# A residual block on one core: RMSNorm scales moved behind the projections, x in column blocks, early transposes of the second norm

## Chip, cores and metric

One core of one Trainium2 chip runs the whole block in one launch. The metric is the device time of the launch in microseconds (us), the median of three runs.

## The reference

`x` is 256 rows (tokens) by 2048 columns, float32.

```
n1   = rmsnorm(x) * g1
proj = n1 @ w_in            # q k v o (4 x 1024), i f (8), x_r g_r (2 x 1024)
A    = sigmoid(o) * headnorm(mlstm(q, k, v, i, f))       # 4 heads x 256
B    = rglru(conv4(x_r)) * gelu(g_r)                     # 8 blocks x 128
x    = x + [A, B] @ w_out
n2   = rmsnorm(x) * g2
gate, up = split(n2 @ w_up)                              # 2 x 5632
x    = x + (silu(conv3(gate)) * up) @ w_down
y    = rmsnorm(x) * g3
```

`rmsnorm(x)` is `x * r`, with one number `r = 1/sqrt(mean(x*x) + eps)` per row. Since `r` belongs to a row of x and not to a column of a weight, `(r*x*g) @ w` equals `r * ((x*g) @ w)`.

## The kernel before

Each float32 operand is used as a rounded part (`hi`) and a rest (`lo`). A 512 KB block of weights (a *unit*) lands in one of four slots of `raw`; ScalarE rounds it into `w[..., 0, :]` (`round_units`), VectorE subtracts to get `w[..., 1, :]` (`split_units`, L550), and TensorE multiplies (`unit`, L946 and L948: one 512-wide and one 256-wide matmul for each pair, 8 pairs in a unit). Four units make a *group*: 256 output columns over the whole depth of 2048. SyncE loads the next unit into a slot as soon as its split is done.

The order of the work on every engine is written out by hand; semaphores that count the named steps of an engine (`Steps`, `after`, `did`) tie them together, and each engine works its own list strictly in order. So what stands behind a waiting instruction waits too.

**Start.** SyncE loads x in five row pieces, then weights. ScalarE squares each piece with a running sum (`squares`), and takes the root of it (`std`); VectorE takes the reciprocal (`norm_scale`) and writes `xn = x * r` (`normalise`, L587). TensorE meanwhile multiplies ones 29 times (L971), then transposes `xn` in eight banks of four 128x128 blocks (`transpose_bank`, L927): banks 0 to 3 ahead of the first group, 4 to 7 inside it (`first_group`). ScalarE and VectorE evacuate each bank as `hi` and `lo` with the gain g1 (`transposed_hi`, `transposed_lo`, L593). Then come group 0 (q), the gate columns i and f (L978, 16 matmuls), and group 1 (k).

**Gate chain.** From the gate columns VectorE and ScalarE compute the running sums and maxima of the gates on 4 rows: `gate_bias`, `gate_sum` (L643), `f_neg`, `f_abs` on VectorE; `f_exp`, `f_ln` on ScalarE, each behind a load of its function table; then on VectorE `logf`, the scan `fsum`, `gdif` (TensorE transposes it, L984), the scan `cmax`, `neg_M`, `neg_m`, `neg_clip`. Only behind `neg_clip` does VectorE's list have the splits of group 2, the v columns of head 0 (L942 on TensorE).

**Heads.** Four rounds of six groups (v, o, x_r, g_r, next q, next k). After each group the two parts are added (`copy_half` on ScalarE, `add_half` L561 on VectorE). The last head's final steps run beside the first units of the output projection.

**Output projection and second norm.** `contraction` runs two halves of the 2048 output columns; a half is four *bodies* of four units (L1051, 12 matmuls for each unit). In PSUM, half 0 uses banks 4 to 7, half 1 banks 0 to 3. VectorE adds the result to x (`add_residual`, L794: `out0_0`, `out1_0` after half 0; `out0_1`, `out1_1`, `out1_2` after half 1). Then the same norm, scaling and transposing as at the start, and the first group of the up projection. Its 22 rounds have two groups each, `gate_post` (conv on VectorE, L845 and L849, silu on ScalarE) and `up_post` (L856).

Of the kernel before, what the change touches and what calls it, by code (L numbers as in the profile page):

```python
# [89 lines left out]
WARM_UP = 29  # L90
# [19 lines left out]
def hybrid_block(nc, x, w_in, w_out, w_up, w_down, wa, wx, gate_w, par_in, const_in, gfin_in, out):  # L110
    with ExitStack() as ctx:
# [3 lines left out]
        def sb(name, shape, dt=F32, where=ctx):  # L115
# [14 lines left out]
        ones = sb("ones", [P, P])  # L130
        ident = cst[:, C_ID:C_ID + P]
# [13 lines left out]
        decay = sb("decay", [P, 3 * P], where=mixer)  # L145
        pT = sb("pT", [P, 3 * P], where=mixer)
# [43 lines left out]
        x_landed = {(r, n): sem(f"x_landed{r}_{n}") for r in range(ROWS) for n in range(len(PIECES[r]))}  # L190
        par_landed = sem("par_landed")
        gate_landed = sem("gate_landed")
# [15 lines left out]
        stats_act = "warm sq0_0 sq1_0 sq0_1 std0 "  # L208
        norm_dve0 = "rstd0 xn0_0 xn0_1 xn0_2 xn0_3 "
        norm_dve1 = "rstd1 xn1_0 xn1_1 xn1_2 "  # L210
        tr_steps = " ".join(f"t{b}" for b in range(KT // 2)) + " "
        norm_act = "sq1_1 sq1_2 std1 t0 t1 t2 t3 xn1_3 t4 t5 t6 t7 "
        out_steps = "out0_0 out1_0 base out0_1 "
        A0 = Steps(act_step, 0, stats_act + norm_act + "gw_hi lam_exp lam_ln gate_half f_exp f_ln floor")
        V0 = Steps(dve_step, 0, "start gw_zero base rstd0 xn0_0 xn0_1 base1 xn0_2 xn0_3 " + norm_dve1 + tr_steps + "gw_lo lam_neg lam_abs lam_relu softplus c_col"
                   " half_bias nc_col hg gate_bias gate_sum f_neg f_abs logf fsum gdif cmax neg_M neg_m neg_clip gcol0 gcol1 pads")
        E0 = Steps(pe_step, 0, tr_steps + "gates gcol0 gcol1")
        A1 = Steps(act_step, A0.end(), "decay hsq rms_std o_tanh r_tanh0 r_tanh1 i_tanh0 i_tanh1 lru_a0 lru_a1 lru_t0 lru_t1 lru_s g_tanh")
        V1 = Steps(dve_step, V0.end(), "arg0 arg1 pT dneg den dsq hvar"
                   " conv0_0 conv1_0 conv0_1 conv1_1 conv0_2 conv1_2 conv0_3 conv1_3 rstd og mix0 mix1"  # L220
                   " ux asq w u scan0 scan1 gsq gp gq gh mixl")
        E1 = Steps(pe_step, E0.end(), "scores pv rms lru")
        L1 = Steps(pool_step, 0, "mask0 mask1 nsq")
        EO = Steps(pe_step, E1.end(H), "row0_0 row0_1 row1_1")
        A2 = Steps(act_step, A1.end(H), stats_act + norm_act)
        V2 = Steps(dve_step, V1.end(H), out_steps + norm_dve0 + "out1_1 out1_2 base1 " + norm_dve1 + tr_steps + "fpad")
        E2 = Steps(pe_step, EO.end(), tr_steps)
        A3 = Steps(act_step, A2.end(), "silu")
        V3 = Steps(dve_step, V2.end(), "c0_0 c1_0 c0_1 c1_1 c0_2 c1_2 act")
        ED = Steps(pe_step, E2.end(), "row0_0 row0_1 row1_1")  # L230
        A4 = Steps(act_step, A3.end(UP_ITERS), stats_act + "y0_0 y0_1 sq1_1 sq1_2 std1 y1_0 y1_1")
        V4 = Steps(dve_step, V3.end(UP_ITERS), out_steps + "rstd0 y0_2 y0_3 out1_1 out1_2 base1 rstd1 y1_2 y1_3")
        L4 = Steps(pool_step, L1.end(H), "xg0 xg1")
# [20 lines left out]
        def _(sp):  # L254
            for r, n in ((0, 0), (1, 0), (0, 1), (1, 1), (1, 2)):
                lo, hi = PIECES[r][n]
                sp.dma_start(xres[:, r, lo:hi], x[0, r * P:(r + 1) * P, lo:hi]).then_inc(x_landed[r, n], 16)
# [9 lines left out]
            def load_group(group, view, col):  # L267
                for s in range(RING):
                    load(group, s, view[s, :, :, bass.ds(col, COLS)],
                         raw[:, s, :].rearrange("p (c n) -> p c n", c=CH))  # L270
# [25 lines left out]
            load_group(0, in_v, COL_Q)  # L296
# [21 lines left out]
        def _(act_e):  # L318
# [20 lines left out]
            def squares(A, r, n, V=None):  # L339

                if V:
                    after(act_e, V, f"out{r}_{n}")
                else:
                    act_e.wait_ge(x_landed[r, n], 16)
# [13 lines left out]
            def stats(A, V, r, source=None):  # L358

                for n in range(1, len(PIECES[r])):  # L360
                    squares(A, r, n, source)
                std(A, V, r)
# [4 lines left out]

            def normalise(A, c):

                cols = slice(c * BANK, (c + 1) * BANK)  # L370
                did(act_fn(xn[:, 1, cols], xres[:, 1, cols], scale=small[:, RSTD + 1:RSTD + 2]), A, f"xn1_{c}")
# [10 lines left out]
            def normalised_hi(A, V, E, gains, prepare):  # L382

                for s in range(RING):
                    prepare(s)
                    if s == 2:
                        after(act_e, V, "rstd1")
                        normalise(A, 3)
                    transposed_hi(A, E, gains, 2 * s)
                    transposed_hi(A, E, gains, 2 * s + 1)  # L390

            after(act_e, V0, "start")
            warm_sqrt(A0)
            for r in range(ROWS):
                squares(A0, r, 0)
            for r in range(ROWS):
                stats(A0, V0, r)
            act_e.wait_ge(par_landed, 32)
            normalised_hi(A0, V0, E0, PAR_GMIX, lambda s: round_units(0, [s]))
            act_e.wait_ge(gate_landed, 16)  # L400
            after(act_e, V0, "gw_zero")
            did(act_fn(gws[:, :, 0:2, 0:H], gw[:]), A0, "gw_hi")

# [4 lines left out]
            round_units(1)  # L408
            copy_half(0, 0, qT[:])
# [76 lines left out]
            def contraction(src, first_group, bodies, A, V):  # L486

                for half in range(2):
                    base = first_group + half * bodies + 1
                    if half == 1 or src is not mixT:  # L490
                        for s in range(RING):
                            round_units(base, [s])
                            round_tiles(src, RING, [s])
# [631 lines left out]
```

## Time and profile before

| | |
|---|---|
| median of three runs | 1156.99 us (1156.61 to 1157.96) |
| span of the profiled execution, first to last instruction | 1146.2 us |
| TensorE busy | 1129.4 us, 99% |
| VectorE busy | 725.4 us, 63% |
| ScalarE busy | 585.5 us, 51% |
| GpSimd busy | 17.4 us, 2% |
| moved by DMA | 213.55 MB, mean 186 GB/s |
| ScalarE function table loads | 25, 1283 ns each |

The runs are timed from outside and are 10.8 us longer than the span of the profiled execution, for which no outside time of its own is given. A busy TensorE here means that matmuls are under way, not that they run at the full clock: PEclk in the profile tells the clock that it was granted, 1.00 for 2.4 GHz and 0.50 for 1.2 GHz. The idle time of an engine only matters where TensorE waits for it.

### The profile page before, as it was taken

To read this page: it belongs to the slowest core of one execution; us is meant where nothing else is said; L and a number is where in the kernel's file an instruction comes from. 1 tells how busy PE (TensorE), PEld (TensorE's weight loads), DVE (VectorE), ACT (ScalarE), POOL (GpSimd) and SP (SyncE) were. 2 spreads that over 40 slices of the span, in tenths; PEclk is the share of its full clock that TensorE was granted. 3 is DMA by queue.
4 is the path that set the end of the run, shared out by engine and by line. 5 is a ranking of instruction groups with operands and counts; after the bars stand their busy time and mean duration, and the time that the engine had idled before them with its cause. 6 is when DMAs were issued, how large, how long until landed. Compare 5 with 4: busy or idle time off the path is not lost.

```text
span 1146.2 us, 18127 instructions
## 1 busy us (share of the span) xinstructions
PE 1129.4 (99%) x6052; PEld 976.8 (85%) x6052; DVE 725.4 (63%) x956; ACT 585.5 (51%) x767; POOL 17.4 (2%) x27
## 2 busy tenths in 40 slices
PE   8999999999999999999999999999999999999997
PEld 7888888888888888888888888888888888888885
DVE  6659576585785586666656656666665755556554
ACT  6647465474665564445444444444444554555454
POOL 0000000000000000000000000000000000002000
PEclk8999999999999999999999999999999999999999
DMA  7665757657565546655665666566565566665653
GB/s 229 197 191 172 196 148 209 165 155 204 183 209 193 167 147 203 194 188 172 207 189 165 212 189 184 180 202 187 168 214 187 193 190 196 189 196 186 195 190 109
DMA packets 165592, 213.55 MB, mean 186 GB/s; under 512 B 6764, under 2 KB 148076, under 8 KB 165440
## 3 DMA queue, kind: packets, MB, share of 16 engines
q1 hardware_dynamic: 164944, 210.79, 59.7%
q0 software_dynamic: 624, 2.45, 0.6%
q8 instruction: 14, 0.23, 0.1%
q14 instruction: 10, 0.08, 0.0%
HBM read 211.10 MB, written 2.11 MB: 186 GB/s over the span
## 4 chain that ended last, share of the span: by engine, by line
PE 97%; ACT 1%; DVE 1%; DMA 1%; issue 0%; DVEq 0%; SPq 0%; ACTq 0%
PE ps L946 41%; PE ps L1051 27%; PE ps L948 21%; PE ps L942 3%; PE ps L944 1%; PE ps L927 1%; DMA xres<-x_dram 1%; PE ps L1022 1%; ACT xn L322 0%; PE ps L978 0%; ACT w L322 0%; PE ps L1004 0%; PE ps L994 0%; DVE aT L556 0%; DVE xn L587 0%
## 5 line engine op out<-in xcount | busy, mean ns | idle before, releaser
L946 PE MATMUL ps<-xT,w 128*128 128x512 f32 x2048 | 716.8, 394 | 0.0
L550 DVE TENSOR_TENSOR w<-raw,w 128x1024 fp32r<-128x1024 f32 x392 | 475.1, 1224 | 366.3 <-ACT w L322 365.5
L322 ACT ACTIVATE w<-raw 128x1024 fp32r<-128x1024 f32 x392 | 411.7, 1058 | 424.7 <-PE ps L948 260.1
L948 PE MATMUL ps<-xT,w 128*128 128x256 f32 x2048 | 573.5, 280 | 0.0
L946 PEld LDWEIGHTS ps<-xT,w 128*128 128x128 f32 x2048 | 384.1, 188 | 85.6
L948 PEld LDWEIGHTS ps<-xT,w 128*128 128x128 f32 x2048 | 387.5, 189 | 0.3
L1051 PE MATMUL ps<-w,aT 128*128 128x512 f32 x1440 | 327.1, 389 | 0.4 <-DVE aT L556 0.4
L1051 PEld LDWEIGHTS ps<-w,aT 128*128 128x128 f32 x1440 | 270.1, 188 | 57.0 <-DVE aT L556 0.9
L322 ACT ACTIVATE fs<-fc 128x512 f32<-128x512 f32 x22 | 13.9, 632 | 86.5 <-DVE fc L849 86.5
L942 PE MATMUL ps<-w,xT 128*128 128x512 f32 x128 | 45.1, 397 | 0.0
L556 DVE TENSOR_TENSOR aT<-act,aT 128x256 fp32r<-128x256 f32 x88 | 39.0, 443 | 0.0
L849 DVE SCALAR_TENSOR_TENSOR fc<-fg,par,fc 128x256 f32<-128x256 f32 x88 | 36.7, 479 | 0.0
L944 PE MATMUL ps<-w,xT 128*128 128x256 f32 x128 | 35.7, 279 | 0.0
L322 ACT ACTIVATE aT<-act 128x256 fp32r (+1 forms) x88 | 35.3, 401 | 0.0
L322 ACT ACT_TABLE_LOAD x25 | 32.1, 1283 | 1.2 <-PEq L1116 0.8
L942 PEld LDWEIGHTS ps<-w,xT 128*128 128x128 f32 x128 | 24.0, 188 | 5.8
L944 PEld LDWEIGHTS ps<-w,xT 128*128 128x128 f32 x128 | 24.1, 188 | 0.0
L322 ACT ACTIVATE xn<-xres 128x1024 f32<-128x1024 f32 (+1 forms) x15 | 13.3, 884 | 19.3 <-DVE xres L794 13.7
L845 DVE TENSOR_SCALAR fc<-fg,par 128x256 f32<-128x256 f32 x44 | 16.2, 410 | 5.9 <-DVE fg L561 5.8
L856 DVE TENSOR_TENSOR act<-fu,fs 128x512 f32 (+1 forms) x22 | 15.2, 693 | 4.9 <-DVE fu L561 4.8
L927 PE MATMUL ps<-cst,xn 128*128 128x128 f32 x64 | 10.9, 336 | 7.0 <-DVE xn L587 7.0
L322 ACT ACTIVATE xT<-ps,par 128x256 fp32r<-128x256 f32 x32 | 12.8, 475 | 8.2 <-PE ps L927 8.2
(131 smaller groups left out, 362.9 us busy)
## 6 DMA issues: line engine op xcount, KB each, us to landing
raw<-w_up_dram SPq DMA_DIRECT2D x176, 512.0 KB, 4.5
raw<-w_in_dram SPq DMA_DIRECT2D x96, 512.0 KB, 3.8
raw<-w_down_dram SPq DMA_DIRECT2D x88, 512.0 KB, 4.6
raw<-w_out_dram SPq DMA_DIRECT2D x32, 512.0 KB, 4.7
y_dram<-xn SPq DMA_DIRECT2D x8, 256.0 KB, 3.0
xres<-x_dram SPq DMA_DIRECT2D x3, 512.0 KB, 6.8
bc<-rows POOLq DMA_DIRECT2D x4, 256.0 KB, 5.4
gfin<-gfin_dram POOLq DMA_DIRECT2D x1, 1024.0 KB, 9.1
```

The costliest lines, as they stand in the source:

```text
L322: return sc.activation(out_, in_, fn, **kw)
L550: v.tensor_tensor(w[:, s, :, 1, :], raw[:, s, :].rearrange("p (c n) -> p c n", c=CH), w[:, s, :, 0, :], ALU.subtract).then_inc(lo_ready, 1)
L556: v.tensor_tensor(aT[:, s, 1, :], src[:, bass.ds(first + s, 1), :].rearrange("p a n -> p (a n)"), aT[:, s, 0, :], ALU.subtract).then_inc(a ...
L845: did(v.tensor_scalar(fc[:, b, :], tap, fpar(b, k), fpar(b, FTAPS), ALU.mult, ALU.add), V3, f"c{b}_{k}")
L849: did(v.scalar_tensor_tensor(out=fc[:, b, :], in0=tap, scalar=fpar(b, k), in1=fc[:, b, :], op0=ALU.mult, op1=ALU.add), V3, f"c{b}_{k}")
L856: did(v.tensor_tensor(act[:, bass.ds(j * 2, 2), :], fu[:], fs[:], ALU.mult), V3, "act")
L927: ins = nc.tensor.transpose(ps[:, 4 + b % 4, n * S + r * P:n * S + (r + 1) * P], xn[:, r, kt * P:(kt + 1) * P], ident)
L942: mm(full, xT[:, kt, 0, cut], w[:, s, c, :, :].rearrange("p a n -> p (a n)"), start=kt == 0, stop=False)
L944: ins = mm(rest, xT[:, kt, 1, cut], w[:, s, c, 0, :], start=False, stop=kt == KT - 1)
L946: mm(full, w[:, s, c, 0, cut], xT[:, kt, :, :].rearrange("p a n -> p (a n)"), start=kt == 0, stop=False)
L948: ins = mm(rest, w[:, s, c, 1, cut], xT[:, kt, 0, :], start=False, stop=kt == KT - 1)
L1051: ins = mm(ps[:, bank0 + 2 * r + n, :], aT[:, s, a_part, cut], w[:, s, 2 * n:2 * n + 2, w_part, :], start=opens and s == 0 and a_part == 0 ...
```

## The change

1. x comes in four column blocks of 512 columns, both halves of the rows in one 512 KB transfer, alternating in SyncE's list with the four units of group 0. The identity matrix and the parameters are issued by ScalarE and no longer by GpSimd; the triangular mask is loaded apart.
2. TensorE transposes `xres` (x itself) as each block lands; 8 in place of 29 matmuls of ones stand ahead. The squares come after the rounding of group 0 on ScalarE, and `r` is ready later.
3. `r` is spread to all partitions by two matmuls of ones with a diagonal matrix (`diagonals`, `spread_rows`, into `rB`): in the middle of group 1, and after the first group of the up projection.
4. The projection outputs are multiplied by `r`: q and k through the decay mask (`rmask`, one GpSimd product of 384 columns for two of 128), v in its two evacuations (now two pieces each), o on GpSimd (`o_r`), x_r and g_r on VectorE (`xr_r`, `gr_r`, 128x512), the gates by `gate_r` and `gate_b`; in the up projection the gate columns on VectorE (`fr`, 128x512) and the up columns through silu's output on GpSimd (`fs_r`).
5. Before the second norm, banks 0 to 3 are transposed after body 1 of half 1, the first rows of banks 4 to 7 inside its last body, their second rows after the first unit of the up projection.

```diff
-WARM_UP = 29
+WARM_UP = 8
...
-            load_group(0, in_v, COL_Q)
+            load_group(0, in_v, COL_Q, load_x)
...
+            def diagonals(A, V):
+                for r in range(ROWS):
+                    after(dve, A, f"std{r}")
+                    did(v.reciprocal(small[:, RSTD + r:RSTD + r + 1], small[:, STD + r:STD + r + 1]), V, f"rstd{r}")
+                for r in range(ROWS):
+                    after(dve, V, f"rstd{r}")
+                    did(v.tensor_scalar(diag[:, r, :], ident, small[:, RSTD + r:RSTD + r + 1], None, ALU.mult), V, f"diag{r}")
+            def row_scales(V, E):
+                after(dve, E, "rB")
+                did(v.tensor_copy(rB[:, 0, :], ps[:, B_DEN, 0:S]), V, "rB")
+                after(dve, V, "rB")
...
+            transpose_x(0)
+            transpose_x(1)
+            pe.wait_ge(group_free, 1)
+            unit(0, 0, 0, tiles=V0)
+            transpose_x(2)
+            unit(0, 1, 0, tiles=V0)
+            transpose_x(3)
+            unit(0, 2, 0, tiles=V0)
+            unit(0, 3, 0, tiles=V0)
...
+            for s in range(RING):
+                unit(1, s, 1)
+                if s == 1:
+                    spread_rows(V0, E0)
...
+                did(v.tensor_tensor(xr[:, :, TAPS - 1:], xr[:, :, TAPS - 1:], rB[:].to_broadcast([P, 2, S]), ALU.mult), V1, "xr_r")
...
+                did(v.tensor_tensor(gr[:], gr[:], rB[:].to_broadcast([P, 2, S]), ALU.mult), V1, "gr_r")
...
+                did(v.tensor_tensor(fg[:, :, FTAPS - 1:], fg[:, :, FTAPS - 1:], rB[:].to_broadcast([P, 2, S]), ALU.mult), V3, "fr")
...
+            with pool.Fori(0, UP_ITERS) as j:
+                after(pool, A3, "silu", j)
+                did(nc.gpsimd.tensor_tensor(fs[:], fs[:], rB[:].to_broadcast([P, 2, S]), ALU.mult), L3, "fs_r")
...
+            contraction(G_OUT, OUT_BODIES, 0, G_OUT, E2, transpose_early, transpose_late)
+            after(pe, V2, "out0_1")
+            unit(G_UP, 0, 0, tiles=V2)
+            after(pe, V2, "out1_2")
+            for b in range(4, 8):
+                did(transpose_bank(b, [1]), E2, f"t{b}")
+            for s in range(1, RING):
+                unit(G_UP, s, 0, tiles=V2)
+            spread_rows(V2, E2)
```

Two places show how the order moves. First VectorE in the gate chain. Before, behind the splits of group 1 (L550; L561 adds q's two parts, L640 and L643 are the gate sums):

```order
L550 TENSOR_TENSOR w<-raw,w 128x4x256 x4
L561 TENSOR_TENSOR qT<-ps,qT 128x512
L640 SCALAR_TENSOR_TENSOR grow<-ps,par,grow 64x256
L643 TENSOR_TENSOR grow<-ps,grow 64x256
L645 TENSOR_SCALAR gtmp<-grow 4x256
L647 TENSOR_TENSOR gtmp<-gtmp,grow 4x256
```

and in the changed kernel, where L572 is the split, L583 the add, L608 the copy of `rB`, L660 to L664 the first steps on the recurrence's parameters, whose result ScalarE waits for:

```order
L572 TENSOR_TENSOR w<-raw,w 128x4x256 x2
L583 TENSOR_TENSOR qT<-ps,qT 128x512
L608 COPY rB<-ps 128x256
L651 TENSOR_SCALAR rmask<-rB,small 128x256
L652 TENSOR_SCALAR rmask<-rB,small 128x128
L656 TENSOR_TENSOR rmask<-rmask,cst 128x128 x2
L660 TENSOR_SCALAR lp<-par 128x8
L662 TENSOR_TENSOR lp<-lp,par 128x8
L664 TENSOR_SCALAR lp<-lp 128x8
L668 TENSOR_TENSOR grow<-ps,grow 64x256
L670 TENSOR_TENSOR grow<-ps,grow 64x256
L672 TENSOR_TENSOR grow<-grow,rB 64x256
```

The gate sums now stand behind the copy of `rB`, five operations of the mask and three on parameters; the splits of group 2 stand behind all of them, as before.

Second, TensorE around the end of the output projection. Before, half 1 ends with its last body (L1051), and all first 16 transposes (L927) follow it:

```order
L1068 COMPARE_AND_BRANCH
L1051 MATMUL ps<-w,aT 128x512 x48
L927 MATMUL ps<-cst,xn 128x128 x16
L946 MATMUL ps<-xT,w 128x512
L948 MATMUL ps<-xT,w 128x256
```

In the changed kernel L1125 is the projection and L985 the transpose:

```order
L1125 MATMUL ps<-w,aT 128x512 x144
L985 MATMUL ps<-cst,xres 128x128 x16
L1145 UNCONDITIONAL_BRANCH
L1125 MATMUL ps<-w,aT 128x512 x48
L1145 REGISTER_ALU
L1145 COMPARE_AND_BRANCH
L1125 MATMUL ps<-w,aT 128x512 x36
L985 MATMUL ps<-cst,xres 128x128 x8
L1125 MATMUL ps<-w,aT 128x512 x12
L1011 MATMUL ps<-xT,w 128x512
L1013 MATMUL ps<-xT,w 128x256
```

Sixteen transposes stand two bodies earlier, eight inside the last body, and the first unit of the up projection (L1011, L1013) follows the projection directly.

## Rows read from the trace of the kernel before

**Rows 1.** Waits of TensorE: engine, line, what for: us in total, times, longest.

```profile
PE ps L927 <- DVE xn L587: 7.0, 2, 4.2
```

**Rows 2.** Timeline, TensorE, start: start us, us, line, operation, count [idle before <-releaser].

```profile
14.46 3.65 PE L927 MATMUL ps<-cst,xn 128*128 128x128 f32 x16 [4.25 <-DVE xn L587]
...
18.54 0.63 PE L946 MATMUL ps<-xT,w 128*128 128x512 f32 x1
...
19.18 0.52 PE L946 MATMUL ps<-xT,w 128*128 128x512 f32 x1
...
21.39 1.04 PE L927 MATMUL ps<-cst,xn 128*128 128x128 f32 x8
22.18 0.47 PE L946 MATMUL ps<-xT,w 128*128 128x512 f32 x1
...
31.51 3.83 PE L978 MATMUL ps<-xT,gws 128*128 128x512 f32 x16
35.18 0.39 PE L946 MATMUL ps<-xT,w 128*128 128x512 f32 x1
```

**Rows 3.** Timeline, ScalarE, start: squares of x, then one evacuation and one rounding.

```profile
8.02 1.06 ACT L322 ACTIVATE xn<-xres 128x1024 f32<-128x1024 f32 x1 [1.42 <-DMA xres<-x_dram]
...
10.20 1.06 ACT L322 ACTIVATE xn<-xres 128x1024 f32<-128x1024 f32 x1 [1.03 <-DMA xres<-x_dram]
...
22.03 1.57 ACT L322 ACTIVATE xT<-ps,par 128x256 fp32r<-128x256 f32 x4 [0.79 <-PE ps L927]
23.47 1.07 ACT L322 ACTIVATE w<-raw 128x1024 fp32r<-128x1024 f32 x1
```

**Rows 4.** Stretches of the windows view: PE, PEld, DVE, ACT, POOL busy; PEclk; DMA share; GB/s.

```profile
12.20:12.70 0.50, 0.00 (x0) 0.00 (x0) 0.50 (x2) 0.50 (x3) 0.00 (x0) 0.91 1.11 350
19.40:19.90 0.50, 0.50 (x4) 0.42 (x4) 0.50 (x3) 0.50 (x2) 0.00 (x0) 0.97 0.02 4
408.00:409.00 1.00, 1.00 (x6) 0.85 (x5) 1.00 (x2) 1.00 (x3) 0.00 (x0) 0.72 0.92 292
```

**Rows 5.** Timeline, ScalarE, gate chain.

```profile
38.39 0.42 ACT L322 ACTIVATE gtmp<-gtmp 4x256 f32<-4x256 f32 x1 [1.34 <-DVE gtmp L647]
38.83 1.28 ACT L322 ACT_TABLE_LOAD   x1
```

**Rows 6.** Timeline, VectorE, gate chain and the splits behind it.

```profile
37.16 0.43 DVE L643 TENSOR_TENSOR grow<-ps,grow 64x256 f32<-64x256 f32 x1
...
43.86 3.48 DVE L550 TENSOR_TENSOR w<-raw,w 128x1024 fp32r<-128x1024 f32 x3
```

**Rows 7.** Timeline, TensorE, first group of head 0.

```profile
46.58 0.50 PE L942 MATMUL ps<-w,xT 128*128 128x512 f32 x1
```

**Rows 8.** Timeline, TensorE, end of the output projection and second norm.

```profile
398.72 3.11 PE L1051 MATMUL ps<-w,aT 128*128 128x512 f32 x13
404.57 0.63 PE L927 MATMUL ps<-cst,xn 128*128 128x128 f32 x4 [2.74 <-DVE xn L587]
...
420.90 0.39 PE L946 MATMUL ps<-xT,w 128*128 128x512 f32 x1
```

**Rows 9.** Timelines, last head: the tile that the second body needs, and the projection.

```profile
324.27 0.42 DVE L556 TENSOR_TENSOR aT<-mixT,aT 128x256 fp32r<-128x256 f32 x1
...
314.57 15.64 PE L1051 MATMUL ps<-w,aT 128*128 128x512 f32 x68
```

**Rows 10.** VectorE groups by shape: busy us, mean ns, idle before.

```profile
L760 DVE TENSOR_TENSOR gr<-gr 128x512 f32<-128x512 f32 x4 | 2.8, 693 | 0.1
```

**Rows 11.** Timelines, GpSimd beside VectorE in the down projection.

```profile
1033.91 5.75 POOL L910 TENSOR_TENSOR xn<-xres,gfin 128x1024 f32<-128x1024 f32 x2 [741.61 <-ACT xn L322]
...
1037.32 2.63 DVE L556 TENSOR_TENSOR aT<-act,aT 128x256 fp32r<-128x256 f32 x1
```

**Rows 12.** Timelines, up projection: VectorE splits and ScalarE rounding.

```profile
450.47 3.50 DVE L550 TENSOR_TENSOR w<-raw,w 128x1024 fp32r<-128x1024 f32 x3 [1.65 <-ACT w L322]
...
454.38 1.06 ACT L322 ACTIVATE w<-raw 128x1024 fp32r<-128x1024 f32 x1 [1.71 <-PE ps L948]
```

More of the change, by code:

```diff
@@ new lines, in hybrid_block @@
+        A0 = Steps(act_step, 0, "warm " + early + "t4 t5 gw_hi t6 t7 " + x_squares + "gate_half lam_exp lam_ln f_exp f_ln floor")
+        V0 = Steps(dve_step, 0, "start gw_zero " + early + "t4 t5 gw_lo t6 t7 base base1 " + rows + "rm0 rm1 tri0 tri1"
+                   " lam_neg lam_abs lam_relu gate_mid gate_sum gate_r gate_b f_neg f_abs softplus c_col"
+                   " half_bias nc_col hg logf fsum gdif cmax neg_M neg_m neg_clip gcol0 gcol1 pads")
+        E0 = Steps(pe_step, 0, early + late + "gates rB gcol0 gcol1")
@@ L222, in hybrid_block @@
         E1 = Steps(pe_step, E0.end(), "scores pv rms lru")
[L223 to L227, printed above, removed]
+        L1 = Steps(pool_step, 0, "mask o_r nsq")
+        E2 = Steps(pe_step, E1.end(H), "row0_0 " + early + "row0_1 row1_1 " + late + "rB")
@@ L228, in hybrid_block @@
+        A2 = Steps(act_step, A1.end(H), "warm sq0_0 sq1_0 " + early + "sq0_1 sq1_1 sq1_2 " + late + "std0 std1")
+        V2 = Steps(dve_step, V1.end(H), "out0_0 out1_0 " + early + "base out0_1 out1_1 out1_2 base1 fpad " + late + rows)
         A3 = Steps(act_step, A2.end(), "silu")
-        V3 = Steps(dve_step, V2.end(), "c0_0 c1_0 c0_1 c1_1 c0_2 c1_2 act")
+        V3 = Steps(dve_step, V2.end(), "fr c0_0 c1_0 c0_1 c1_1 c0_2 c1_2 act")
+        L3 = Steps(pool_step, L1.end(H), "fs_r")
         ED = Steps(pe_step, E2.end(), "row0_0 row0_1 row1_1")
-        A4 = Steps(act_step, A3.end(UP_ITERS), stats_act + "y0_0 y0_1 sq1_1 sq1_2 std1 y1_0 y1_1")
@@ L484, in _, with prepare_body @@
             head(H - 1, True)
+            def prepare_body(src, group, first):
+                for s in range(RING):
+                    round_units(group, [s])
+                    round_tiles(src, first, [s])
             def contraction(src, first_group, bodies, A, V):
@@ L489, in contraction @@
                     base = first_group + half * bodies + 1
[L490 to L493, printed above, removed]
+                    prepare_body(src, base, RING)
                     if half == 1:
@@ L1067, in contraction @@
                     body(0, opens=True)
-                    with pe.Fori(1, bodies - 1) as b:
+                    if half == 1 and early:
+                        body(1)
+                        early()
+                    with pe.Fori(2 if half == 1 and early else 1, bodies - 1) as b:
                         body(b)
```

316 lines of the change are left out of this document (179 added, 137 removed).

## Prediction

> **What bounds the kernel now.** I read the waits of TensorE first. It is busy for 99% of the span and waits for work twice, 7.0 us together, both times for a normalised x to transpose: 4.2 us at the start, 2.7 us at the second norm [rows 1, 8]. Nearly everything between is a queue of matmuls without a gap. So work added on VectorE, ScalarE or GpSimd costs only where TensorE comes to wait for it, and there are three places to look at: the start, the gate chain, the second norm. Second I read the timelines of these places, third the granted clock in the windows view. TensorE waited from 10.2 to 14.46; from about 12.6 its clock was 1.2 GHz, half of the full one (mean 0.91 of a stretch of 0.5 us), and it came back only at about 19.4, some 4.9 us after work began again [rows 2, 4]. At half clock a pair of matmuls takes 0.64 us (18.54 to 19.18), at full clock 0.35; a unit of 8 pairs is 2.8 us (group 1 and the two small gcol transposes run from 35.18 to 46.58) [rows 2, 7]. At the second norm the clock fell again and was back at about 408.5, 4.0 us after the restart at 404.57 (0.72 as the mean of 408 to 409) [rows 4, 8].
>
> **Start.** Removed from the path: squares, root and scaling, between the last piece of x and the first transposes. Their place is taken by the landing of column blocks 0 and 1. SyncE now has block 0, a unit of weights, block 1 in its list. The second and third 512 KB pieces landed at 8.02 and 10.20 before [rows 3]; block 1 is the third, so I take 10.20. TensorE then has 8 transposes at half clock (half of 16 in 3.65: 1.8 us), to 12.0. It is unit 0's turn, long rounded and split. The clock should be back 4.9 us after 10.2, at 15.1: five pairs of 0.64, three of 0.35, to 16.3. Eight warm transposes are 0.8 us (21.39 to 22.18) [rows 2], to 17.1; unit 1 to 19.9; the last transposes to 20.7; unit 2 to 23.5. Unit 3 waits a little: bank 6 is there at 20.3, its and bank 7's evacuation takes 1.57 us, the rounding 1.07 [rows 3], the split 1.2 [rows 6], to 24.1. Unit 3 ends at 26.9, the 16 gate matmuls take 3.7 us (31.51 to 35.18), and group 1 begins at 30.6 in place of 35.18 [rows 2]: **4.6 us earlier**. The 21 matmuls of ones that go cost nothing where they stood, but the clock is no longer full at 10.2; that is in the sum, since the first transposes were slow before as well. The transfers move four blocks past units of weights; block 3, now the seventh of eight pieces, is not wanted before 19.9, so the four pieces after the third have 9.7 us.
>
> **Gate chain.** Here the change adds a wait. `rB` comes out of TensorE between units 1 and 2 of group 1: 5.6 us after its start, and about 0.4 for the two small matmuls, so at 36.6. Call this R. It needs `diag1`: ScalarE is through with unit 3 at about 23, has three 1.06 us squares, two of 0.6, two roundings and two roots to do, some 8.5 us, and `diag1` follows at about 32.3, 4 us early. Behind R stand in VectorE's list: the copy (0.43, as L643 [rows 6]), four operations for the mask (0.3 each), two small ones (0.2 each): 2.0 us. Then ScalarE: `lam_exp`, table load 1.28, `lam_ln`, table load 1.28, to R + 5.0; the gate sums on VectorE, six operations of about 0.43, are done at R + 4.6. From the start of `f_exp` to the end of the first split of group 2 it was 6.7 us (38.39; first of three splits from 43.86, 1.2 us) [rows 5, 6], and this piece is unchanged. So the first unit of head 0 can start at R + 11.7 = 48.3, while TensorE is through with group 1 at R + 5.6. Before, it started at 46.58 [rows 7] without a wait. The lead of 4.6 us is gone and **1.7 us are lost** on top. The wait is 6.1 us, broken only by two tiny transposes when `gdif` comes; the clock fell in the shorter waits, so it falls here, and 4.0 to 4.9 us at half clock cost 2.0 to 2.5: **2.2 us**. Who else waits: ScalarE's `floor` and GpSimd's `bc` transfers come about 3 us later, but `arg0`, which wants them, follows TensorE's own delay of 3.9.
>
> The page "ScalarE: Activation LUTs" of the Trainium skill, What ACT_TABLE_LOAD costs, gives about 1.28 us for a load plus about 1.38 for a drain. By the page, the three loads of this chain behind R would cost 4.1 us more. The trace speaks against it: `f_exp` ends at 38.81 and the load begins at 38.83 [rows 5]. I take 1.28 alone.
>
> **Heads.** v: two pieces for one, 0.3 us on VectorE; the mask: one GpSimd operation for two; both end 7 us before TensorE asks. `o_r` on GpSimd has a whole group of 11 us. `xr_r` and `gr_r` are 0.69 us each [rows 10] and 0.7 with their wait, 1.4 a head. In three heads VectorE's list has idle places that take in the first, and the next splits come about a microsecond ahead. In the last head it runs without a pause into the output projection: the tile for body 1 was ready at 324.69, would be at 326.1, and TensorE wants it at 325.6 (48 matmuls of 0.23 us behind 314.57) [rows 9]. **0.5 us lost**; bounds 0 and 1.4.
>
> **Second norm.** From the last projection matmul (401.83) to the second group of the up projection (420.90) it was 19.1 us [rows 8]. Of the new list, all of this stands on TensorE: 32 transposes at full clock, 3.2; four units, 11.2; two matmuls for `rB`, 0.4; 14.8 in all. Gaps should not come: `out1_0` is long done when body 1 ends; `out0_1` (1.2 us) has two half units, 2.7 us; `out1_2` is covered by the first unit, 2.8 us, and banks 4 to 7 are evacuated beside unit 1. **4.3 us gained**; the lower bound, with half a unit of gap, is 2.9.
>
> **Up projection.** `fr` adds 0.7 us to VectorE in each of 22 rounds. The split of the first unit of the next even group ended at 451.7 and TensorE took it at about 454.4 (the end of a group, which ScalarE's rounding at 454.38 waited for) [rows 12]; 2.0 us of 2.7 stay. `fs_r` on GpSimd begins when silu ends and is wanted by `act` more than 6 us later. Two GpSimd products of 1024 columns took 5.75 us, 2.9 each; a 512-wide one is some 1.4 by that. A VectorE subtraction beside them took 2.63 us in place of 0.42, and ended when GpSimd did [rows 9, 11]. So `fs_r` may hold up a split by 0.3 us, since the rounding before it takes 1.1 of the 1.4. Zero cost. The Trainium skill's page "SBUF — State Buffer", Who interferes with whom, calls this an exclusive lock of the port pair that GpSimd shares with VectorE, held for an instruction; the trace agrees, 2.63 us for 0.42.
>
> **Sum.** +1.7 + 2.2 + 0.5 - 4.3 = +0.1 us on the span of 1146.2. The runs' median is 10.8 us above the span, and nothing outside the span changes: 1156.99 + 0.1 = **1157.1 us**. Two large gains and two large losses cancel, so the error of each stays in full. A measurement of this kernel tells 0.2%, 2.3 us, from no change.
>
> **Rivals.**
> - *x early.* Block 1 lands like the second piece, at 8.0: 2.2 us less, 1154.9. For it: the parameters leave GpSimd's queue and compete less at once. Against: it is third in the list. With smaller gains elsewhere it passes the limit of 1154.7.
> - *Clock stays.* The two gcol transposes, or the shortness of each part of the gap (3.1 and 2.7 us), keep the clock full: 2.2 us less, 1154.9; with x early, 1152.7. Against: it fell with waits of 4.3 and 2.7 us.
> - *x late (slower).* Interleaved with weights in short rows, block 1 lands a piece later, at 12.4. TensorE has nothing else, so each microsecond counts in full: 1159.3. It decides from a landing at 12.4 on.
> - *Gap at the second norm (slower).* ScalarE, whose list has squares and roundings between, brings the evacuation of banks 4 to 7 late, and the old gap with its clock loss (2.7 + about 1) stays: 1160.8.
> - *Table loads as the page has them.* 4.1 us on the gate chain: 1161.2. Against: the row in [rows 5].
> - *GpSimd's lock.* `fs_r` takes longer beside VectorE than my 1.4 us. From 3.1 us on (2.7 - 0.7 + 1.1) the splits come too late; 0.3 us beyond that in 22 rounds are 7 us: 1164. Against: even a product twice as wide took 2.9 [rows 11].
> - *The scales don't hide in the heads.* 1.4 us lost in each of four heads for 0.5 in the last: 1162.2.
>
> **How the numbers follow.** The forecast, within 2.3 us: 0.51. x early 0.13, clock stays 0.10, x late 0.10, gap 0.06, loads 0.03, lock 0.04, heads 0.03. Of the two early cases, half go below 1154.7. Of the forecast's own error 0.04 falls on either side of the limits. Faster: 0.04 + 0.12 = 0.16, and 0.02 for both early cases at once: 0.18. Slower: 0.04 + 0.10 + 0.06 + 0.10 = 0.30. Same: 0.52. The range leaves out the rarest: 1153.8 (both early cases in part) to 1161.2 (gap, loads).
>
> **What would show it.** Group 1 starts near 30.6 and the clock comes back near 15; TensorE has one wait of about 6 us, in two parts, ahead of the first v unit at about 48.3, with PEclk 0.5 behind it; a wait of half a microsecond at body 1; none at the second norm, with the second up group 3.8 us (+4.3 - 0.5) closer to the start of the projection; no waits in the up projection, and VectorE 0.7 us busier in each round. A wait missing ahead of the v unit, or group 1 later than 33, would make this wrong.

## The result and the profile after

The changed kernel takes 1147.84 us (median of 20 runs, 1146.49 to 1148.44). In the same comparison the kernel before took 1156.74 us (20 runs, 1146.87 to 1157.96). The ratio is 0.9946, with a 95% interval of 0.9927 to 0.9965: faster by half a per cent, where I forecast no change at 1157.1 us, and below my range of 1153.8 to 1161.2.

The median hides how the runs of before lie. They form two groups with nothing between. In all comparisons of this study together, 65 of 174 runs lie between 1146.4 and 1148.8 (mean 1147.8) and 109 between 1155.8 and 1158.2 (mean 1157.1). All runs of the changed kernel lie in one group, mean 1147.7. Below, "short" and "long" are these groups.

The profiled execution of the changed kernel took 1147.8 us by its own time, 1.9 us more than its span of 1145.9. (In every run of the experiments below this difference lies between 1.7 and 1.9 us.) With as much around it, the profiled execution of before, span 1146.2, would have taken 1148: it was a short one, beside a median of three long ones. Its units of the up projection run at the pace of the short runs, as shown further down.

From the page of the changed kernel, engines' busy time, and the group of the new GpSimd products:

```profile
PE 1126.4 (98%) x6018; PEld 968.7 (85%) x6018; DVE 750.3 (65%) x988; ACT 581.8 (51%) x769; POOL 51.8 (5%) x48
...
L969 POOL TENSOR_TENSOR fs<-fs,rB 128x512 f32<-128x512 f32 x22 | 28.6, 1299 | 569.4 <-ACT fs L330 569.4
```

Waits of TensorE in the changed kernel (total, times, longest), which answer to [rows 1]:

```profile
PE ps L1058 <- DVE gdif L695: 3.1, 1, 3.1
PE ps L1007 <- DVE w L572: 2.6, 1, 2.6
PE ps L985 <- DMA xres<-x_dram: 2.3, 2, 1.8
PE ps L1024 <- DVE small L633: 1.4, 1, 1.4
PE ps L1125 <- DVE aT L578: 0.9, 2, 0.5
PE ps L1011 <- DVE w L572: 0.7, 1, 0.7
PE ps L1011 <- issue: 0.6, 1, 0.6
```

The two waits for a normalised x are gone. In their place stand 2.3 us for x itself and 5.7 us in the gate chain (`gdif`, then the split for the first v unit). No wait is left at the second norm, and the up projection has none. Of the two waits for `aT`, one is at body 1 of the output projection (0.46 us, at 329.15) and one in the down projection (0.44 us, at 1039.66); the second was there before as well:

```profile
1040.00 0.74 PE L1051 MATMUL ps<-w,aT 128*128 128x512 f32 x2 [0.44 <-DVE aT L556]
```

Timeline of TensorE in the changed kernel, for [rows 2, 7, 8, 9]:

```profile
9.11 1.09 PE L985 MATMUL ps<-cst,xres 128*128 128x128 f32 x8 [1.81 <-DMA xres<-x_dram]
10.76 0.77 PE L1011 MATMUL ps<-xT,w 128*128 128x512 f32 x1 [0.56 <-issue]
...
26.07 3.84 PE L1048 MATMUL ps<-xT,gws 128*128 128x512 f32 x16
35.38 0.60 PE L993 MATMUL ps<-diag,ones 128*128 128x128 f32 x4
44.61 0.37 PE L1058 MATMUL ps<-cst,gdif 4*128 4x4 f32 x2 [3.07 <-DVE gdif L695]
47.54 0.79 PE L1007 MATMUL ps<-w,xT 128*128 128x512 f32 x1 [2.55 <-DVE w L572]
...
317.63 11.07 PE L1125 MATMUL ps<-w,aT 128*128 128x512 f32 x48
329.15 54.70 PE L1125 MATMUL ps<-w,aT 128*128 128x512 f32 x240 [0.46 <-DVE aT L578]
...
405.30 2.98 PE L1125 MATMUL ps<-w,aT 128*128 128x512 f32 x12
...
408.12 0.39 PE L1011 MATMUL ps<-xT,w 128*128 128x512 f32 x1
...
420.13 0.61 PE L993 MATMUL ps<-diag,ones 128*128 128x128 f32 x4
...
420.49 0.47 PE L1011 MATMUL ps<-xT,w 128*128 128x512 f32 x1
```

The gate matmuls begin at 26.07 where they began at 31.51 [rows 2]; the first v unit at 47.54, after 46.58 [rows 7]; the output projection at 317.63, after 314.57 [rows 9]; the second up group at 420.49, after 420.90 [rows 8]. So the changed kernel gains, loses, and is 0.4 us ahead at 420, about as it is at the end (spans 1145.9 and 1146.2). Between executions of the same pace the change is worth nothing that can be measured (the short runs of before have a mean of 1147.8 us, the changed kernel 1147.7). What it did was to end the long runs.

Windows of the changed kernel (columns as in [rows 4]):

```profile
10.00:11.00 1.00, 0.44 (x3) 0.27 (x2) 0.99 (x2) 1.00 (x4) 0.00 (x0) 0.61 1.03 380
...
13.50:14.50 1.00, 1.00 (x7) 0.87 (x7) 0.08 (x1) 0.00 (x0) 0.00 (x0) 0.93 1.06 364
...
45.00:50.00 5.00, 2.46 (x7) 2.13 (x8) 4.90 (x8) 4.05 (x5) 0.52 (x1) 0.50 0.23 44
...
51.00:52.00 1.00, 1.00 (x7) 0.88 (x7) 0.77 (x4) 0.00 (x0) 0.00 (x0) 0.91 0.98 348
```

The clock fell to 1.2 GHz in both gaps and came back near 13.5 and 51.

### The profile page after: what moved, and what is told of

It is laid out like the page before. It is cut to its first block, busy times and chain, and to the rows that moved or that the text cites. A ratio compares the mean times of both kernels' runs of the same rounds, so it can differ in the third digit from the quotient of the medians.

```text
span 1145.9 us, 18106 instructions
## 1 busy us (share of the span) xinstructions
PE 1126.4 (98%) x6018; PEld 968.7 (85%) x6018; DVE 750.3 (65%) x988; ACT 581.8 (51%) x769; POOL 51.8 (5%) x48
## 4 chain that ended last, share of the span: by engine, by line
PE 94%; DVE 4%; ACT 1%; DMA 1%; issue 1%; SPq 0%; DVEq 0%; ACTq 0%
PE ps L1011 40%; PE ps L1125 27%; PE ps L1013 20%; PE ps L1007 3%; PE ps L1009 1%; DVE w L572 1%; DMA xres<-x_dram 1%; PE ps L985 1%; PE ps L1096 0%; DVE aT L578 0%; PE ps L1048 0%; PE ps L1078 0%; PE ps L1068 0%; ACT w L330 0%; ACT xn L330 0%
## 5 line engine op out<-in xcount | busy, mean ns | idle before, releaser
L1011 PE MATMUL ps<-xT,w 128*128 128x512 f32 x2048 | 717.5, 396 | 1.2 <-DVE w L572 0.7
L572 DVE TENSOR_TENSOR w<-raw,w 128x1024 fp32r<-128x1024 f32 x392 | 480.4, 1238 | 344.1 <-ACT w L330 343.5
L1013 PE MATMUL ps<-xT,w 128*128 128x256 f32 x2048 | 569.7, 278 | 0.0
L1011 PEld LDWEIGHTS ps<-xT,w 128*128 128x128 f32 x2048 | 384.8, 188 | 91.1 <-DVE w L572 1.0
L1013 PEld LDWEIGHTS ps<-xT,w 128*128 128x128 f32 x2048 | 385.8, 188 | 0.3
L1125 PE MATMUL ps<-w,aT 128*128 128x512 f32 x1440 | 327.9, 389 | 0.9 <-DVE aT L578 0.9
L1125 PEld LDWEIGHTS ps<-w,aT 128*128 128x128 f32 x1440 | 269.8, 188 | 57.7 <-DVE aT L578 1.7
L969 POOL TENSOR_TENSOR fs<-fs,rB 128x512 f32<-128x512 f32 x22 | 28.6, 1299 | 569.4 <-ACT fs L330 569.4
L623 DVE SCALAR_TENSOR_TENSOR xT<-ps,par,xT 128x256 fp32r<-128x256 f32 x32 | 13.1, 478 | 8.8 <-ACT xT L330 8.7
```

The lines of the kernel that those rows point to most:

```text
L572: v.tensor_tensor(w[:, s, :, 1, :], raw[:, s, :].rearrange("p (c n) -> p c n", c=CH), w[:, s, :, 0, :], ALU.subtract).then_inc(lo_ready, 1)
L969: did(nc.gpsimd.tensor_tensor(fs[:], fs[:], rB[:].to_broadcast([P, 2, S]), ALU.mult), L3, "fs_r")
L1011: mm(full, w[:, s, c, 0, cut], xT[:, kt, :, :].rearrange("p a n -> p (a n)"), start=kt == 0, stop=False)
L1013: ins = mm(rest, w[:, s, c, 1, cut], xT[:, kt, 0, :], start=False, stop=kt == KT - 1)
L1125: ins = mm(ps[:, bank0 + 2 * r + n, :], aT[:, s, a_part, cut], w[:, s, 2 * n:2 * n + 2, w_part, :], start=opens and s == 0 and a_part == 0 ...
```

## The experiments

First came the question where the 9 us between the groups lie, then what turns one into the other, and beside it what parts of the change are worth.

**1. The kernel before, unchanged**, with a profile of a long run.

> The kernel before, unchanged, to see its two groups of times (14 of 20 near 1157, 6 near 1147.5) with a span and a clock for each run. Theory A (queue): in the long runs the identity and the parameters, which GpSimd issues, land some 10 us later, and TensorE waits for them: the spans of long runs are 10 us longer, the clock near the same. Theory B (clock): the spans are 10 us longer and the mean clock is lower by about 0.01 (20 us at half of it). Theory C (outside): all spans are near 1146.2, and the 10 us lie outside the first and last instruction.

Three runs short (1147.8 to 1148.3), nine long (1156.2 to 1157.8). This profile is of a long one: time 1157.17, span 1155.3, again 1.9 us around it. The difference lies within the span. It is not the clock either, since the mean granted clock is 0.994 here, as in the three short runs, and 0.993 in the profile after. The groups by shape show it. TensorE between 440 and 880 us, where nothing but the up projection runs and TensorE never idles: kernel before, short execution:

```profile
L946 PE MATMUL ps<-xT,w 128*128 128x512 f32 x1271 | 440.7, 391 | 0.0
L948 PE MATMUL ps<-xT,w 128*128 128x256 f32 x1270 | 355.6, 280 | 0.0
```

the same kernel, long execution:

```profile
L946 PE MATMUL ps<-xT,w 128*128 128x512 f32 x1247 | 440.6, 399 | 0.0
L948 PE MATMUL ps<-xT,w 128*128 128x256 f32 x1246 | 349.9, 281 | 0.0
```

and the changed kernel:

```profile
L1011 PE MATMUL ps<-xT,w 128*128 128x512 f32 x1271 | 440.7, 394 | 0.0
L1013 PE MATMUL ps<-xT,w 128*128 128x256 f32 x1270 | 351.8, 277 | 0.0
...
440.00:880.00 440.00, 440.00 (x2541) 384.80 (x2540) 293.65 (x359) 194.22 (x219) 25.98 (x20) 1.00 0.61 188
```

In the same 440 us, at a granted clock of 1.00 and with no idle time of TensorE in either, 24 pairs fewer pass in the long run. A pair takes 0.3463 us (440/1270.5) or 0.3530 (440/1246.5); over the 176 units of 8 pairs of the up projection that is 1408 x 0.0067 = 9.4 us, the distance of the groups. The starts of ScalarE's rounding, one for each unit, give 2.773 or 2.827 us a unit from the second round to the last. So this form of pair has **two paces**, and one of them is kept through the whole up projection.

The heads have the same two paces. In all 20 profiles the pace turns in each of the four heads, from one to the other, at the eight matmul instructions of the recurrence's gates (L1022 before, L1096 after). In the changed kernel a group of 32 pairs takes 11.31 us in the second head (starts at 99.17, 110.48 and 121.79) and 11.10 in the third (172.37, 183.47). In the heads the turns all but cancel; in the up projection nothing turns the pace back. And the pace of the last head doesn't choose that of the up projection: in the changed kernel the last six groups ahead of the output projection are slow, in number 18 they are fast, and the up projection is fast in both.

**2. and 3. Who issues the parameters.** Only the changed kernel issues them on ScalarE, so a queue could have been the cause. Before with ScalarE:

```diff
+            act_e.dma_start(cst[:], const_in).then_inc(par_landed, 16)
+            act_e.dma_start(par[:], par_in).then_inc(par_landed, 16)
-            pool.dma_start(cst[:], const_in).then_inc(par_landed, 16)
-            pool.dma_start(par[:], par_in).then_inc(par_landed, 16)
```

> The kernel before, with only the constants and the parameters issued by ScalarE in place of GpSimd. Theory A: all runs are near 1147 to 1148, none near 1157. Theories B and C: two groups as before, most runs near 1157.

Six runs short, six long (1146.7 to 1148.3, 1156.0 to 1157.6). And the changed kernel with `ident` and `par` on GpSimd:

```diff
-            act_e.dma_start(ident, const_in[:, C_ID:C_ID + P]).then_inc(ident_landed, 16)
-            act_e.dma_start(par[:], par_in).then_inc(par_landed, 16)
+            pool.dma_start(ident, const_in[:, C_ID:C_ID + P]).then_inc(ident_landed, 16)
+            pool.dma_start(par[:], par_in).then_inc(par_landed, 16)
```

> The changed kernel, with only the identity and the parameters back on GpSimd's queue. Theory A: most runs go up by about 10 us, to 1157 or 1158. Theories B and C: all runs stay near 1147.8.

One group, 1147.4 to 1151.3, median 1149.5; TensorE waits 1.9 us for the identity. The queue doesn't choose the pace; the place of these loads is worth some 1.7 us in the median.

**4. Warm-up.** Before with `WARM_UP = 8`.

> The kernel before with 8 matmuls of ones in place of 29. Theory B (the long row of ones matmuls brings the clock into a longer half-clock stretch): near 1147 in all runs. Theories A and C: two groups as before.

Five short, seven long; the short ones as fast as before. The 21 matmuls are worth nothing, as the prediction had it.

**5. No clock fall at the second norm.** In before, matmuls of ones take the first part of the wait there:

```diff
+            after(pe, V2, "out1_0")
+            for n in range(15):
+                mm(ps[:, B_DEN, 0:P], ones[:], ones[:], start=True, stop=True)
```

> The kernel before with 15 matmuls of ones (30 records of about 0.08 us, 2.5 us) in front of the transposes of the second norm, so that the wait of 2.7 us there is nearly filled and the clock stays full. Theory Clock: the two paces of the up projection (2.77 and 2.83 us a unit, 176 units, 9.4 us) are drawn when the clock comes back from half to full; then all runs fall in one group, and with the half-clock loss of about 1.7 us saved they are near 1145.5 (or near 1155 if the one pace is the slow one). Theory Wait: they are drawn at any wait of TensorE there; two groups remain, at about 1145.5 and 1155. Theory Start: they are drawn at the start; two groups remain too.

Three short, nine long. The windows of a long run show a clock that never fell:

```profile
404.00:410.00 6.00, 5.38 (x43) 4.95 (x42) 5.53 (x11) 4.05 (x11) 0.00 (x0) 1.00 0.26 87
440.00:880.00 440.00, 440.00 (x2492) 381.44 (x2492) 270.49 (x333) 191.01 (x214) 0.00 (x0) 1.00 0.59 185
```

2492 matmuls, the slow pace: the clock's fall isn't what chooses it. A wait of 0.6 us for `xT` was left. The 1.7 us that I expected from the clock didn't come: the short runs took 1146.8 to 1148.4, as before.

**6. The changed kernel without its part 5**: all 32 transposes behind the projection. Of the edit, the lines on TensorE's hooks are shown; the transposes and their evacuations move with them.

```diff
-            contraction(G_OUT, OUT_BODIES, 0, G_OUT, E2, transpose_early, transpose_late)
+            contraction(G_OUT, OUT_BODIES, 0, G_OUT, E2)
...
```

> The changed kernel with part 5 alone undone: all transposes of the second norm stand behind the output projection, four banks before the first unit, two after each of the next two. TensorE waits again, some 2 to 4 us. Theories Clock and Wait: two groups of times come back, 9.4 us apart, the lower 3 to 5 us above 1147.8 (1151 to 1153) and the upper 1160 to 1162. Theory Start: one group, near 1151 to 1153.

Six runs at 1150.6 to 1152.5 (mean 1151.7) and six at 1159.1 to 1161.0. TensorE's timeline:

```profile
405.82 1.97 PE L979 MATMUL ps<-cst,xres 128*128 128x128 f32 x16 [1.58 <-DVE xres L839]
409.26 0.47 PE L1005 MATMUL ps<-xT,w 128*128 128x512 f32 x1 [1.47 <-DVE xT L620]
```

Part 5 does two things: it saves 4.0 us (1151.7 - 1147.7), and it ends the long runs. With the waits at the entrance of the up projection, the two groups are back.

**7. Short matmuls inside the first up group**: four behind the spreading of `rB` in the changed kernel.

```diff
             spread_rows(V2, E2)
+            for n in range(4):
+                mm(ps[:, 6, 0:S], ones[:], diag[:].rearrange("p a n -> p (a n)"), start=True, stop=True)
```

> The changed kernel with four more float32 matmuls of 128x256 behind the two that spread r at the second norm, the same form and number as the recurrence gates, after which the pace of the units changed in each head of every profile. Cost of their own: 1.7 us. Theory Phase (the pace is a phase that such a set of matmuls shifts): the up projection runs at 2.83 us a unit in all runs, near 1159. Rival (the pace depends on nothing that stands in TensorE's list): near 1149.5 in all runs.

One group, 1148.4 to 1150.8, fast pace. They are eight matmul instructions of the same shape as the recurrence's gates, at which the pace turns in every head; here, behind the four instructions that spread `rB`, they didn't turn it. So neither the number nor the shape of the matmuls put in is all that counts.

**8. Splits of group 2 ahead of and within the gate chain** of the changed kernel, and the two gcol transposes behind group 2. VectorE's part of the edit is shown; ScalarE's roundings move likewise, and head 0 stands outside the loop over the heads:

```diff
+            split_units(2, [0])
...
+            split_units(2, [1])
...
+            split_units(2, [2])
...
-            split_units(2)
+            split_units(2, [3])
```

> The changed kernel with the units of group 2 (v of head 0) rounded and split ahead of and inside the gate chain, and the two gcol transposes behind group 2 on TensorE. If the wait of 5.6 us before group 2 and the 3.6 us at half clock behind it are what the gate chain costs, TensorE has no wait there and the time falls by 5.6 + 1.8 = 7.4 us, to about 1140.4. Rival: the chain then holds up the scores of head 0 or the bc transfers, and 3 us or more come back there. The paces of the heads may change as well, by 1 to 2 us either way.

1141.40 us (8 runs, 1140.5 to 1142.6), ratio 0.9898 (0.9864 to 0.9933). TensorE's waits:

```profile
PE ps L989 <- DMA xres<-x_dram: 2.9, 2, 2.5
...
PE ps L1015 <- DVE w L573: 0.6, 1, 0.6
PE ps L1011 <- DVE w L573: 0.5, 1, 0.5
```

The wait for `gdif` is gone, that for the split fell from 2.6 to 0.5 us, and the clock, which fell at 44 us in the changed kernel, stays at 1.00. The gain is 6.3 us by the means of the runs (1147.7 and 1141.4): 5.2 us of waits, and about one more. How much of this last one is the clock isn't shown, as a new wait of 0.3 us stands ahead of the scores.

**9. A wait of 0.8 us, and no other change.** In the changed kernel the wait for `out1_2` goes ahead of the first up unit:

```diff
-            after(pe, V2, "out0_1")
+            after(pe, V2, "out1_2")
             unit(G_UP, 0, 0, tiles=V2)
-            after(pe, V2, "out1_2")
```

> The changed kernel with one wait moved: TensorE waits for out1_2 ahead of the first unit of the up projection, not behind it, so it stands still about 1 us there, at full clock, and nothing else is changed. Theory Wait (a wait of TensorE at the second norm draws the pace of the up projection anew): two groups of times, near 1148.8 and near 1158, of 12 runs at least 3 in each. Rival (what is drawn hangs on the start, on the transposes of the scaled x, or on the clock): one group near 1148.8.

All 12 runs long: 1157.92 (1156.8 to 1158.9), ratio 1.0031 (1.0006 to 1.0056). TensorE's timeline:

```profile
409.76 0.50 PE L1011 MATMUL ps<-xT,w 128*128 128x512 f32 x1 [0.79 <-DVE xres L842]
```

Between 440 and 880 us its profile has 1246 pairs, the slow pace. **A wait of 0.8 us costs 10.1 us**: itself, and 9.4 for the pace. Two groups were expected; it is one.

**10. Before without any wait at the second norm**: 22 matmuls of ones ahead of the 16 transposes, 12 behind.

> The kernel before with 22 matmuls of ones in front of the first 16 transposes of the second norm and 12 behind them, more than its waits there are long, so that TensorE has none. Cost: about 1 to 2 us more matmuls than the waits, less 1.7 us of half clock. Theory Wait: one group of times only, near 1147 or near 1156.5. Rival: two groups 9.4 us apart.

One group, but the slow one: 1160.44 (1159.9 to 1161.1), ratio 1.0059 (1.0032 to 1.0086). So "no wait" means one pace in all runs, not the fast one.

**11. The best version**: number 8, with 8 matmuls of ones between the transposes of blocks 0 and 1.

```diff
             transpose_x(0)
+            for n in range(8):
+                mm(ps[:, B_DEN, 0:P], ones[:], ones[:], start=True, stop=True)
             transpose_x(1)
```

> e8 (the changed kernel with the v units of head 0 early) and 8 matmuls of ones between the transposes of x block 0 and block 1, where TensorE stands 1.8 to 2.5 us. If the half clock of 10.3 to 13.4 comes from this pause, the clock stays or comes back earlier and up to 1.5 us are saved: about 1140 against 1141.4. Rival: the clock comes back at the same time whatever runs there, and the time is the same within 0.5 us, or later if block 1 lands before the ones are through.

**1139.53 us** (6 runs, 1139.1 to 1140.3), ratio 0.9874 (0.9836 to 0.9912). Its timeline:

```profile
6.50 1.95 PE L1043 MATMUL ps<-ones 128*128 128x128 f32 x16
9.23 1.09 PE L989 MATMUL ps<-cst,xres 128*128 128x128 f32 x8 [0.78 <-DMA xres<-x_dram]
10.21 0.47 PE L1015 MATMUL ps<-xT,w 128*128 128x512 f32 x1
```

Eight matmuls of ones are 16 instructions in the trace: each of these float32 products is two. The first unit runs at full clock from its start (0.47 us in place of 0.77), though x lands no earlier. Against number 8 that is worth 1.9 us, a little more than the 1.5 expected.

**12, 13, 15, 18. The number of matmuls of ones directly ahead of the up projection**, in the changed kernel, with no wait; one, five, two and four:

```diff
             after(pe, V2, "out0_1")
+            for n in range(1):
+                mm(ps[:, 1, 0:P], ones[:], ones[:], start=True, stop=True)
             unit(G_UP, 0, 0, tiles=V2)
```

> The changed kernel with one matmul of ones (128x128, into bank 1) between the output projection and the first unit of the up projection, without any wait on another engine. Theory Wait (both paces occur only where TensorE enters the up projection out of a wait): one group of runs. Which pace is open. Theory Slip (the pace is carried in from the matmuls ahead, so any matmul of another length there can turn it, as a count of ones did in the run without waits): all runs at the slow pace, 1157.3 (1147.8 + 0.1 + 9.4). If one matmul doesn't turn it: 1147.9.

> The same with five matmuls of ones. One group of runs again by both theories; 1148.2 at the fast pace (five of 0.06 us), 1157.6 at the slow one. If one matmul and five give different paces, the number of matmuls ahead of the up projection alone chooses it.

> The changed kernel with two matmuls of ones, in place of one, between the output projection and the first unit of the up projection. Theory Parity (an odd number of matmuls put in, one or five, turned the pace, so an even number leaves it): the fast pace in all runs, 1148.0 (1147.8 + 0.2). Theory In-front (any short matmul directly in front of the first unit turns it): the slow pace in all runs, 1157.4.

> The changed kernel with four matmuls of ones between the output projection and the first up unit. Theory Parity (one and five turned the pace, two did not): the fast pace in all runs, 1148.5. Theory Small-offset (the time of arrival decides, and two just happened to fit): 1157.7, or two groups.

| matmuls of ones | median | range, 10 runs each (20 for none) |
|---|---|---|
| 0 | 1147.84 | 1146.5 to 1148.4 |
| 1 | 1157.16 | 1156.5 to 1158.4 |
| 2 | 1148.94 | 1147.7 to 1149.7 |
| 4 | 1148.33 | 1147.4 to 1149.9 |
| 5 | 1158.85 | 1157.9 to 1159.3 |

One and five matmuls (2 and 10 instructions in the trace) turn all runs to the slow pace; none, two and four (0, 4 and 8) leave it. Odd against even is the simplest rule that fits these five counts; no other count was run. With one matmul the shapes between 440 and 880 us read

```profile
L1011 PE MATMUL ps<-xT,w 128*128 128x512 f32 x1247 | 440.7, 399 | 0.0
L1013 PE MATMUL ps<-xT,w 128*128 128x256 f32 x1246 | 349.9, 281 | 0.0
```

and with four there are 1270 pairs.

**14. One more matmul behind the transposes of number 10** (13 for 12).

> The kernel before, filled so that TensorE has no wait at the second norm (22 matmuls of ones ahead of the 16 transposes), with 13 matmuls of ones behind them where the earlier run had 12 and was slow in every run (1160.4). If the count chooses the pace, this can come out at 1151.1 (9.4 us less, 0.06 more); if something farther ahead does, all runs stay at 1160.5. One group of runs in either case.

1160.56 (1159.7 to 1161.1): all slow still. So the rule of odd and even, which fits the five counts at one place of the changed kernel, doesn't hold at the same place of the kernel before, nor in the heads (number 7).

**16. One matmul farther ahead**: before the transposes in the projection's last body, with eight transposes and twelve 512-wide matmuls behind it.

```diff
                     after(pe, V2, f"t{b - 4}")
+                    if b == 4:
+                        mm(ps[:, 4, 0:P], ones[:], ones[:], start=True, stop=True)
```

> The changed kernel with one matmul of ones ahead of the transposes in the last body of the projection, so that the first unit of the up projection still follows the projection's 512-wide matmuls directly. Theory In-front: the fast pace in all runs, 1147.9. Theory Parity: one more matmul turns the pace from wherever it stands, 1157.3 in all runs.

1147.77 (1146.1 to 1149.5): fast. The matmul that turns the pace directly ahead of the first unit doesn't turn it from here. One place was tried, with one matmul.

**17. One matmul behind the wait of number 9.**

> The changed kernel with the wait of 0.8 us ahead of the first up unit (all runs slow, 1157.9) and one matmul of ones behind that wait. Theory Turn (what stands at the entrance only turns the pace from one to the other, and one matmul turns it again): all runs at the fast pace, 1148.7. Theory Wait (a wait at the entrance makes it slow or leaves it open): all runs slow, 1158.0, or two groups.

1158.17; nine runs at 1157.4 to 1159.4, one at 1149.9. One matmul doesn't turn the pace back once a wait stands there. One short run in ten, where number 9 had none in twelve, is too little to say that the matmul let it in; but both paces do occur behind this wait.

**What is settled and what is not.** Shown: the difference is the pace of the pairs in the up projection; TensorE takes it up on entering; a wait there leads to both paces or to the slow one (before and numbers 1, 2, 4, 5, 6, 9, 17); without a wait all runs of a kernel have the same pace (after and 3, 7, 8, 10 to 16 and 18), and in the changed kernel one or five short matmuls directly ahead make it the slow one. Not the cause: the clock, the parameters' queue, the warm-up. Open: what inside TensorE differs between the paces, by what rule short matmuls turn them, and why numbers 10 and 14 are both slow.

## Why the prediction was wrong

**The step that failed** is in the sum: "The runs' median is 10.8 us above the span, and nothing outside the span changes". I took 10.8 us for time around the span, and so as fixed. Number 1 has 1.9 us there. The other 9 were within the span of the long executions, at a place where the profile that I had, of a short one, shows nothing wrong. No rival had such a case: each of them moved a wait, a landing, the clock or the length of some operations. The wait at the second norm that I priced at 4.3 us was worth 4.0 by itself, and some 9.4 us more in five of eight runs, which is what brought the median down.

**The terms of the sum**, for two executions at the same pace in the up projection, have the right signs; those of the v unit and of the clock were 0.7 us too large each, and one was missing:

| step | predicted | in the two profiles |
|---|---|---|
| gate matmuls earlier | 4.6 us | 5.4 (31.51 to 26.07) |
| first v unit later | 1.7 | 1.0 (46.58 to 47.54) |
| half clock behind that gap | 2.2 | 1.5 (first group of head 0 and the scores: 14.09 us for 12.63) |
| pace in the heads | not foreseen | 0.6 (later by 2.4 at 61.63, by 3.1 at the projection) |
| body 1 | 0.5 | 0.5 (one new wait of 0.46 us) |
| second norm | -4.3 | -4.0 (number 6; from -0.4 at 420 less 3.1 and 0.5: -4.0 too) |
| span | +0.1 | -0.3 |

The row of the clock goes by these windows, of the kernel before and of the changed one, from the first v unit to the start of the next group:

```profile
46.58:59.21 12.63, 12.63 (x75) 11.03 (x73) 6.50 (x9) 5.71 (x6) 2.65 (x5) 1.00 1.00 326
...
47.54:61.63 14.09, 14.09 (x73) 12.34 (x73) 7.87 (x10) 5.75 (x7) 2.66 (x5) 0.87 0.97 311
```

The 0.6 us come from the order of the paces: the first head of this profile is fast and that of before slow. In number 18, whose heads have the order of before, the delay is 2.0 us at the second group of head 0 and still 2.0 at the projection (316.57). That the sum for the span came within 0.4 us of the measured one was in part luck: the missing term stood in for what the v unit and the clock cost less than I had priced.

- *Start.* Block 1 landed at 9.11, between my 10.20 and the 8.0 of "x early", and the clock was back near 13.5 and not 15.1. The first v unit came 0.8 us sooner than I had it: 0.6 because `rB` left TensorE at 36.0 and not 36.6, and 0.2 in the chain behind it. "x early" was worth about a third of its price.
- *Gate chain.* From R to the first v unit I had 11.7 us; it was 11.5. The chain of waits ran as written. The rows, VectorE and ScalarE of the changed kernel:

```profile
36.02 0.42 DVE L608 COPY rB<-ps 128x256 f32<-128x256 f32 x1 [3.64 <-PE ps L993]
...
46.28 2.34 DVE L572 TENSOR_TENSOR w<-raw,w 128x1024 fp32r<-128x1024 f32 x2
```

```profile
37.99 1.28 ACT L330 ACT_TABLE_LOAD   x1
39.28 0.21 ACT L330 ACTIVATE lp<-lp 128x8 f32<-128x8 f32 x1
39.51 1.28 ACT L330 ACT_TABLE_LOAD   x1
40.80 0.42 ACT L330 ACTIVATE gtmp<-gtmp 4x256 f32<-4x256 f32 x1
```

  Each load takes 1.28 us and the next operation begins right behind it. The drain of about 1.38 us, which the Trainium skill's page "ScalarE: Activation LUTs", What ACT_TABLE_LOAD costs, adds, doesn't show; "table loads" falls.
- *Clock stays* falls: two small transposes within the gap don't hold it (0.50 from 45 to 50 us). Where numbers 8 and 11 put work in place of the gap, it was 1.00.
- *x late, gap at the second norm, heads* fall: no such waits.
- *GpSimd's lock.* `fs_r` takes 1.30 us for my 1.4. VectorE's splits between 440 and 880 us, before and after:

```profile
L550 DVE TENSOR_TENSOR w<-raw,w 128x1024 fp32r<-128x1024 f32 x160 | 192.5, 1224 | 156.8 <-ACT w L322 156.3
...
L572 DVE TENSOR_TENSOR w<-raw,w 128x1024 fp32r<-128x1024 f32 x159 | 196.3, 1254 | 137.5 <-ACT w L330 137.0
```

  One split in each of the 20 rounds, the one that begins while `fs_r` runs, takes 1.47 to 1.49 us, the others 1.22 to 1.23: 0.25 us for my 0.3, and no wait of TensorE follows. That agrees with the port pair being locked for the length of an instruction, which the Trainium skill's "SBUF — State Buffer", Who interferes with whom, states; other reasons for the delay were not tested.

The range was built from the terms of the span alone, so it missed by the one number that I had not questioned.

## What to carry to other kernels

Check a profiled execution's span against the runs before adding a change to their median: here they were 1.7 to 1.9 us apart for every single run, and where a median is far above that, the profile may be of another kind of run, and the next question is what the runs have that the profile doesn't. A wait just ahead of a long stretch of the same matmuls can cost far more than itself (0.8 us cost 10.1), so it is worth a trial without it; whether the pace behind is then the fast one has to be measured, since number 10 had no wait and was slow. And a chain of small operations on VectorE or ScalarE should let through the splits that stand behind it: that was worth 6.3 us here.

## What the runs showed of the hardware

Not expected: alternating 512- and 256-wide matmuls on new weights run at 0.3463 or 0.3530 us a pair at full clock, 2% apart, for 490 us without a change. A single 128x128 float32 matmul (two instructions in the trace) directly ahead of the first of them turned all ten runs from one to the other, at a cost of 9.3 us (1147.84 to 1157.16), and with a second one all ten were fast again (1148.94). In the heads the pace turned at the recurrence's gate matmuls, 80 times out of 80 in 20 profiles.
